# Last expert of a pass: high half of w_down in two retired gather buffers, split ahead of the SwiGLU

## The reference, cut to what matters

```python
lg = hf @ w_rg + b_rg;  g_top = argmax(lg)               # one group of four
top_v, top_i = top_k(le_sel, 2)                          # two of its eight experts
w2 = softmax(top_v) * p_sel
for g in range(4):                                       # e: the 8 experts of the group, F = 256
    a   = einsum('td,edf->tef', hf, w_gate[g])
    b   = einsum('td,edf->tef', hf, w_up[g])
    act = silu(a) * b * cg[..., None]
    y  += einsum('tef,efd->td', act, w_down[g])
x = x + y;  y_out = rmsnorm(x, g_final)
```

## Time and profile before

| What | us |
|---|---|
| median of 3 runs (lowest, highest) | 1020.39 (1020.3, 1021.37) |
| the profiled execution, its own time | 1020.66 |
| its span | 1018.8 |
| TensorE (PE) busy in the span | 930.5 (91%) |
| VectorE (DVE) busy | 568.8 (56%) |
| ScalarE (ACT) busy | 305.3 (30%) |
| GpSimd (POOL) busy | 90.4 (9%) |

### The profile page before, as it was taken

How to read it: one execution, slowest core, us unless ns; L and a number is a source line. 1 busy time by engine, 2 the same in 40 slices (tenths; PEclk the granted TensorE clock), 3 DMA queues, 4 the chain that set the end, 5 groups by cost and what they waited for, 6 DMA issues and landing times.

```text
span 1018.8 us, 15065 instructions
## 1 busy us (share of the span) xinstructions
PE 930.5 (91%) x6165; PEld 886.9 (87%) x6165; DVE 568.8 (56%) x799; ACT 305.3 (30%) x491; POOL 90.4 (9%) x106
## 2 busy tenths in 40 slices
PE   5999999999999999999999946999999999999810
PEld 4999999999999999998878836999999999999710
DVE  6549878687878554276223372344444444444448
ACT  6521221311111287223022211233232332323323
POOL 0000000100000000000000012223222232221100
PEclk9999999999999999999999966999999999999955
DMA  9021111111112101125124377699999999997157
GB/s 288 3 63 42 42 42 37 32 55 42 52 42 84 42 22 32 32 84 169 45 80 179 120 294 226 245 334 341 348 330 352 349 328 371 342 363 284 28 229 293
DMA packets 77754, 170.16 MB, mean 167 GB/s; under 512 B 10763, under 2 KB 48155, under 8 KB 68449
## 3 DMA queue, kind: packets, MB, share of 16 engines
q1 hardware_dynamic: 68481, 152.05, 42.3%
q0 software_dynamic: 9216, 17.32, 5.1%
HBM read 156.83 MB, written 22.47 MB: 176 GB/s over the span
## 4 chain that ended last, share of the span: by engine, by line
PE 89%; DVE 7%; DMA 2%; issue 1%; ACT 1%; DVEq 0%; SPq 0%; POOLq 0%; ACTq 0%
PE ps L1425 41%; PE ps L1651 23%; PE ps L1635 9%; PE ps L1574 9%; PE ps L1621 2%; DVE x L1390 2%; PE ps L1498 1%; PE ps L1558 1%; DVE x L1401 1%; PE ps L1435 1%; PE ps L1550 1%; PE ps L1492 1%; DMA g_mix_b<-in_g_mix 1%; DMA X<-H,g_now 0%; DMA YK<-Y,s_now 0%
## 5 line engine op out<-in xcount | busy, mean ns | idle before, releaser
L1425 PE MATMUL ps<-hT,w_hi 128*128 128x352 f32 x1344 | 329.6, 326 | 0.0
L1651 PEld LDWEIGHTS ps<-XT,wgu 128*128 128x128 f32 x2048 | 236.5, 194 | 5.2 <-ACT XT L883 2.6
L1651 PE MATMUL ps<-XT,wgu 128*128 128x104 f32 x2048 | 236.4, 277 | 2.2 <-ACT XT L883 2.2
L1425 PEld LDWEIGHTS ps<-hT,w_hi 128*128 128x128 f32 x1344 | 236.2, 189 | 0.7
L1425 PE MATMUL ps<-hT,w_lo 128*128 128x352 f32 x672 | 218.5, 325 | 0.0
L1003 DVE SCALAR_TENSOR_TENSOR C<-V,w_dw,C 128x1086 f32<-128x1086 f32 x120 | 154.8, 1343 | 0.3
L1425 PEld LDWEIGHTS ps<-hT,w_lo 128*128 128x128 f32 x672 | 126.3, 188 | 0.0
L1349 DVE TENSOR_TENSOR wdn_lo<-wdn,wdn_hi 128x1024 fp32r<-128x1024 f32 x64 | 75.5, 1221 | 53.9 <-ACT wdn_hi L905 53.9
L1574 PE MATMUL ps<-wo_hi,hT 128*128 128x512 f32 x288 | 90.6, 396 | 1.2 <-DVE wo_lo L1081 1.2
L938 DVE TENSOR_TENSOR w_lo<-w_raw,w_hi 128x1024 fp32r<-128x1024 f32 (+1 forms) x44 | 45.2, 1027 | 66.3 <-ACT w_hi L696 66.3
L1574 PEld LDWEIGHTS ps<-wo_hi,hT 128*128 128x128 f32 x288 | 53.4, 188 | 13.5 <-issue 1.6
(11 more groups left out here) (211 smaller groups left out, 1113.2 us busy)
## 6 DMA issues: line engine op xcount, KB each, us to landing
wgu<-in_w_gate SPq DMA_DIRECT2D x32, 1024.0 KB, 10.2
wgu<-in_w_up SPq DMA_DIRECT2D x32, 1024.0 KB, 14.6
wdn<-in_w_down SPq DMA_DIRECT2D x32, 1024.0 KB, 10.6
w_raw<-in_w_in SPq DMA_DIRECT2D x28, 512.0 KB, 3.8
yy<-YK SPq DMA_DIRECT2D x8, 1024.0 KB, 12.5
xs<-in_x_prompt SPq DMA_DIRECT2D x8, 512.0 KB, 7.7
wo_raw<-in_w_out SPq DMA_DIRECT2D x8, 512.0 KB, 5.0
xr<-in_x_prompt SPq DMA_DIRECT2D x16, 256.0 KB, 2.6
```

What stands on the lines that cost most here:

```text
L1425: op = pe.matmul(ps[:, bank_of(m, c), 0:CH], a[s][:, k, :], r[:, k, c * CH:(c + 1) * CH], start=(k == 0 and q == 0), stop=(k == K - 1 and ...
L1651: m = pe.matmul(ps[:, 2 + b, o:o + CAP], wgu[u][:, h, c, f * P:(f + 1) * P], XT[:, b, c, 0:CAP], start=(c == 0), stop=(c == KD - 1))
```

## The change

Two buffers `end_hi` are named, at the places of `X[:, 0]` and `X[:, 1]`. For the last expert of a pass alone, ScalarE makes the high part of w_down there, ahead of its SiLU and without the wait for `s_down`, but with a wait for the transposes of that expert (`s_tx`, it+1), since these are the last reads of X. VectorE subtracts ahead of its product AT, and TensorE's last `down` reads `end_hi`. For the other 31 experts the instructions and their order are as before.

```diff
+        end_hi = [at(f"end_hi{c}", [P, D], F32R, r_h + 49152 + c * 4096) for c in range(KF)]
...
+        def last(i, u):
+            return isinstance(i, int) and i == GE // WB - 1 and u == WB - 1
...
+            def down_hi(p, i, u, halves):                          # ScalarE
+                act.wait_ge(s_wl[u], 48 * (p * (GE // WB) + i + 1))
+                for c in range(KF):
+                    op = act.activation(halves[c][:], wdn[u][:, c, :], ACT.Copy)
+                op.then_inc(s_dnhi, 1)
+
             def step(p, i, u):
+                if last(i, u):
+                    act.wait_ge(s_tx, it + 1)
+                    down_hi(p, i, u, end_hi)
                 act.wait_ge(s_gu, it + 1)
...
-                act.wait_ge(s_wl[u], 48 * (p * (GE // WB) + i + 1))
-                wait(act, s_down, it)
-                for c in range(KF):
-                    op = act.activation(wdn_hi[c][:], wdn[u][:, c, :], ACT.Copy)
-                op.then_inc(s_dnhi, 1)
+                if not last(i, u):
+                    wait(act, s_down, it)
+                    down_hi(p, i, u, wdn_hi)
...
+            def down_lo(it, u, halves):                            # VectorE
+                dve.wait_ge(s_dnhi, it + 1)
+                for c in range(KF):
+                    op = dve.tensor_tensor(wdn_lo[u][:, c, :], wdn[u][:, c, :], halves[c][:].bitcast(F32), ALU.subtract)
+                op.then_inc(s_dnlo, 1)
+
             def step(p, i, u):
+                if last(i, u):
+                    down_lo(it, u, end_hi)
                 dve.wait_ge(s_sg, it + 1)
...
-                dve.wait_ge(s_dnhi, it + 1)
-                for c in range(KF):
-                    op = dve.tensor_tensor(wdn_lo[u][:, c, :], wdn[u][:, c, :], wdn_hi[c][:].bitcast(F32), ALU.subtract)
-                op.then_inc(s_dnlo, 1)
+                if not last(i, u):
+                    down_lo(it, u, wdn_hi)
...
-            def down(it, u):                                       # TensorE
+            def down(it, u, halves):
-                        for q, (a, w) in enumerate(((AT_hi, wdn_hi[c][:, cols]), (AT_lo, wdn_hi[c][:, cols]),
+                        for q, (a, w) in enumerate(((AT_hi, halves[c][:, cols]), (AT_lo, halves[c][:, cols]),
...
-                    down(it - 1, (u - 1) % WB)
+                    down(it - 1, (u - 1) % WB, wdn_hi)
...
-                down(p * GE + GE - 1, WB - 1)
+                down(p * GE + GE - 1, WB - 1, end_hi)
```

## The result

| | median, us (lowest to highest, runs) | ratio to the kernel before | span of the profile |
|---|---|---|---|
| before | 1020.54 (1020.3 to 1021.37, 4) | | 1018.8 |
| changed | 1012.94 (1012.64 to 1014.54, 4) | 0.9928 [0.9915, 0.994] | 1010.8 |
| changed, a second time | 1013.82 (1012.66 to 1013.95, 5) | 0.9931 [0.9917, 0.9945] | 1012.1 |

The forecast was 1013.5. All nine runs of the changed kernel together have a median of 1013.19. The kernel before ran beside it each time: 1020.54 in the first comparison and 1020.17 (9 runs) in the second. So the medians differ by 7.60 us in the first and by 6.35 in the second; the ratios, over the same runs, make it 7.3 (6.1 to 8.7) and 7.0 (5.6 to 8.5).

What follows compares the result with a forecast made beforehand. TensorE, busy 91% of the span, bounds the kernel until its stall before `down(31)`, then one chain to the end. Stall 5.05 + clock 1.93 = 6.98 us off the 1020.39 median gives 1013.4; forecast 1013.5, range 1012.5 to 1015.5.

Steps and rivals of the forecast that it cites:

- Split early, margin 2.6 us: ScalarE's two copies for expert 31 run from about 955.2 to 957.2, 2.6 us ahead of SiLU(31).
- Subtraction early, margins 0.26 and 1.3: VectorE's subtraction ends 0.26 us before AT(31) starts; VectorE may be 1.3 us late before TensorE waits.
- The wait on `s_tx` and the new operands at nothing: ScalarE's added wait costs 0 (ends 0 and 0.14 us); `end_hi` in the last 12 matmuls 0 (-0.1 to +0.1).
- The stall, 5.05: TensorE's wait between `down(30)` and `down(31)` goes, as all inputs arrive before 962.61: 5.05 us less.
- `down(31)` at the higher clock, 1.93: Without idle time ahead, TensorE's last `down` takes 2.83 us in place of 4.76: 1.93 less (ends 0 and 1.93).
- The scatter at 4.36: GpSimd's last scatter, starting 2.8 us after the one before, still takes 4.36 us (ends -0.5 and +4.4).
- A: Software transfers are served one after the other; scatter 31 starts 1.07 us later: gain 5.9, time 1014.6; chance 0.05.
- E: Slower: the last two scatters are served in turn at 8.8 us each, 3.4 us more, time 1023.8; chance 0.03.
- The tail as long as before: VectorE's tail after the load of `yy` begins at 975.1 and keeps its length.
- Rival D: Another wait of the same length stands behind the one removed: no gain, time 1020.4; chance 0.03.

Runs made afterwards that it cites:

- buffers_only: The changed kernel with ScalarE's split and VectorE's subtraction back at their old places, new buffers kept; 1020.46 us, ratio 1.0 to the kernel before.
- hi_early_lo_late: The changed kernel with only VectorE's subtraction put back to the end of its step, ScalarE's copies still early; 1017.09 us, ratio 0.9966 to the kernel before.

## Why the prediction was right

- *Split early, margin 2.6 us.* Right: the copies lie where they were put (954.35 on an axis 0.74 early is 955.1), SiLU(31) kept its place.
- *Subtraction early, margins 0.26 and 1.3.* Right. The first was 0.34; the second was tried from both sides, one extra operation free, two not.
- *The wait on `s_tx` and the new operands at nothing.* Nothing of them is seen in the timelines; a price of a few hundredths could not be.
- *The stall, 5.05.* Right to the hundredth: no L1652 row is left among TensorE's waits from 700 us on. The kernel with the buffers alone, which gained nothing, shows that the order gives it and not the buffer.
- *`down(31)` at the higher clock, 1.93.* 1.96 measured (4.76 to 2.80). The cause was a little off: 1.73 by the clock, 0.2 by following on without a pause. In part the size was luck: after the same pause `buffers_only` took 4.56, and from there it would have been 1.76. The ground given for it, that the clock would not fall while TensorE works, held here (1.00 in both windows), where no pause stood ahead. As a rule it does not hold: in `hi_early_lo_late` the clock fell 1.3 to 1.5 us into `down(31)`, behind a pause of 3.19.
- *The scatter at 4.36.* 4.28 in the changed kernel and 4.35 in its second profile, though scatter 31 was issued at 966.33 while scatter 30 was in flight until 963.55 + 4.0 = 967.55. Rivals A and E are out: as A had it the scatter would have landed 1.2 us later, and as E had it each would have taken 8.8. Whether the data of two scatters are moved side by side is not shown: GpSimd was done with scatter 31 at 967.32, only 0.23 us ahead of the landing of scatter 30, and that is less than the scatters differ among themselves. The seven other profiles had 3.83 to 4.61, with no order by the distance of the scatters. The Trainium skill's sentence on a single software queue ("DMA: Bandwidth & Descriptors", section "SWDGE vs HWDGE vs iDMA") doesn't mean that the issue waits for the landing: scatter 31 was issued 1.22 us ahead of the landing of scatter 30.
- *The tail as long as before.* 1010.8 - 974.02 = 36.78 us against 1018.8 - 982.05 = 36.75. The load of `yy` took 3.21 in place of 3.41, by chance as far as is shown.
- *Rival D.* No other wait stood behind: none appeared.

The sum from the last gate and up group on: 7.02 (TensorE) + 0.08 (scatter) + 0.20 (load) less 0.03 (tail), 7.3 with roundings. The forecast had 6.98 for all of it. The medians over all runs differ by 7.2 (1020.43 of 34 runs, 1013.19 of 9), between the 7.6 of the first comparison and the 6.35 of the second. So the 7.02 rests on the profiles, and the medians agree with it to some tenths. The profiled execution of the first comparison had luck in the first group's clock: 0.7 us of its 8.0.

## What to carry to other kernels

At the end of a pipelined loop, look at what the last iteration waits for without any work left to cover it: buffers that earlier iterations have retired can let its preparation run an iteration ahead. The new buffer alone gained nothing, and the move on ScalarE alone removed 1.86 of the 5.05 us; it took the move in the streams of both engines. Count the clock with the stall: here 5.05 us of waiting cost 7.0. Where the wait itself can't be removed, filling it with matmuls that nothing reads gained 2.0 us at the end of this phase and 3.9 at its start. When the span moves by more than the change explains, compare the two traces stage by stage before the extra is credited to it.

## What was not expected of the hardware

After a pause of 3.19 us the granted clock had stayed at 1.00 through the pause, and fell 1.3 to 1.5 us into the work that followed (matmuls 0.23 us apart, then 0.43); after 1.10 us it did not fall. In two pauses of 5.05 us it fell some 2 us into the one and at the end of the other. Each of these is one profile. A group of 12 matmuls of 512 columns takes 3.03 to 3.06 us after a pause and 2.80 to 2.83 without one, at the same clock. And the point at which the clock rises at the start of the expert phase moved the first group by 1.5 us between two executions of one program (9.06 and 10.55).
